# The order of two attention kinds inside one mixer: dilated groups first, latent groups last

## What is computed

```python
z = rmsnorm(x, mix_norm_ab) @ w_in_ab              # 672 latent columns | 2304 dilated columns
# latent attention (MLA), 8 heads
cq, ckv, k_rope = split(z[:, :672], [384, 640])
cq, ckv = rmsnorm(cq, q_norm), rmsnorm(ckv, kv_norm)
q = cq @ w_uq        # 8 heads x (64 plain + 32 turned by the rotary angles)
k_nope, v = ckv @ w_ukv                             # 8 heads x (64 | 64)
k = [k_nope, rope(k_rope) for every head]
o_a = softmax(q k^T / sqrt(96)) v                   # 512 columns
# dilated attention, 3 dilations x 4 slots
o_g, lse_g = softmax(q_g k_g^T / 8 + bias_g) v_g
o_b = sum_g softmax_g(lse) o_g                      # 256 columns
x = x + [o_a, o_b] @ w_out_ab
```

## Time and profile before

| | us |
|---|---|
| median of 3 runs | 2044.84 (2043.64 to 2045.15) |
| the profiled execution, its own time | 2039.9 |
| its span in the trace | 2038.1 |
| busy: PE | 1965.0 (96%) |
| busy: DVE | 1379.5 (68%) |
| busy: ACT | 838.4 (41%) |
| busy: POOL | 105.3 (5%) |

### The profile page before, as it was taken

One profiled execution on the slowest core, in us unless ns is written; L12 is line 12 of the kernel. 1 busy time (PEld: TensorE's weight loads), 2 busy tenths in 40 slices (PEclk: granted clock), 3 DMA queues, 4 the chain that ended last, 5 costly groups with the idle time before them and its releaser, 6 DMA issues.

```text
span 2038.1 us, 33547 instructions
## 1 busy us (share of the span) xinstructions
PE 1965.0 (96%) x12752; PEld 1773.3 (87%) x12752; DVE 1379.5 (68%) x1758; ACT 838.4 (41%) x1043; POOL 105.3 (5%) x130
## 2 busy tenths in 40 slices
PE   7989999989999999999999999999999999999998
PEld 7978888878888888899899988878888998998886
DVE  5477776766777776755576777777667457677776
ACT  4454333544333433334254343333334325534333
POOL 0002000410000000000100100000000002010000
PEclk9999999999999999999799999999999999999999
DMA  7503555414555555545333455565554443344553
GB/s 286 186 40 123 194 190 187 175 42 180 194 194 190 214 196 185 188 153 181 110 112 138 166 176 189 195 229 188 186 188 174 162 148 104 125 172 170 186 190 139
DMA packets 47761, 343.60 MB, mean 169 GB/s; under 512 B 5360, under 2 KB 5392, under 8 KB 7456
## 3 DMA queue, kind: packets, MB, share of 16 engines
q1 hardware_dynamic: 44784, 324.55, 44.4%
q0 software_dynamic: 2864, 17.46, 2.3%
HBM read 340.94 MB, written 1.05 MB: 168 GB/s over the span
## 4 chain that ended last, share of the span: by engine, by line
issue 65%; PE 28%; POOL 3%; DVE 3%; ACT 1%; DMA 0%; POOLq 0%; DVEq 0%; ACTq 0%
PE bank L820 8%; PE bank L704 4%; PE bank L706 4%; PE bank L705 4%; PE bank L819 4%; PE bank L763 1%; PE bank L895 1%; PE bank L871 1%; POOL rstd L596 1%; DVE y L1439 1%; POOL mix L694 1%; PE bank L822 0%; POOL gn L644 0%; POOL grs L596 0%; POOL rnorm L686 0%
## 5 line engine op out<-in xcount | busy, mean ns | idle before, releaser
L1402 DVE TENSOR_TENSOR wlo<-raw,whi 128x2048 fp32r<-128x2048 f32 x306 | 701.2, 2293 | 301.3 <-ACT whi L1110 300.2
L820 PE MATMUL bank<-ysp,whi 128*128 128x512 f32 x2112 | 731.8, 397 | 6.3 <-DVE ysp L1417 4.1
L1110 ACT ACTIVATE whi<-raw 128x2048 fp32r<-128x2048 f32 x307 | 586.2, 1909 | 283.9 <-PE bank L706 279.4
L819 PE MATMUL bank<-ysp,wlo 128*128 128x256 f32 x1848 | 516.1, 279 | 0.0
L820 PEld LDWEIGHTS bank<-ysp,whi 128*128 128x128 f32 x2112 | 382.1, 188 | 81.5 <-issue 6.0
L819 PEld LDWEIGHTS bank<-ysp,wlo 128*128 128x128 f32 x1848 | 349.2, 189 | 11.8
L1175 ACT ACTIVATE sg<-sg 128x256 f32<-128x256 f32 x132 | 55.2, 418 | 505.2 <-DVE sg L1496 505.2
L704 PE MATMUL bank<-ysp,wlo 128*128 128x256 f32 x720 | 210.3, 292 | 9.9 <-ACT gates L1343 8.0
L705 PE MATMUL bank<-ysp,whi 128*128 128x256 f32 x720 | 207.1, 288 | 0.0
L706 PE MATMUL bank<-ysp,whi 128*128 128x256 f32 x720 | 207.0, 287 | 0.0
L704 PE MATMUL bank<-whi,hl 128*128 128x512 f32 x528 | 205.6, 389 | 0.0
(11 more groups left out here) (292 smaller groups left out, 2415.3 us busy)
## 6 DMA issues: line engine op xcount, KB each, us to landing
raw<-stream SPq DMA_DIRECT2D x307, 1024.0 KB, 4.8
gbc<-gains POOLq DMA_DIRECT2D x11, 512.0 KB, 4.0
cw<-small POOLq DMA_DIRECT2D x2, 2048.0 KB, 10.8
dbias<-dilb POOLq DMA_DIRECT2D x1, 2304.0 KB, 10.2
lng<-rows POOLq DMA_DIRECT2D x2, 1024.0 KB, 5.2
tab<-second POOLq DMA_DIRECT2D x1, 1724.0 KB, 9.3
x<-xin SPq DMA_DIRECT2D x2, 512.0 KB, 6.6
out<-y SPq DMA_DIRECT2D x1, 1024.0 KB, 3.8
```

Source lines behind the costliest of these rows:

```text
L819: pe.matmul(o[:, 0, :], lo[:, k, cols], yh[:, k, :], start=False, stop=False, skip_group_check=True)
L820: last = pe.matmul(o, hi[:, k, cols], ysp[:, :, k, :], start=k == 0, stop=k == 7)
L1110: act.activation(whi[s], raw[s], ACT.Copy).then_inc(hi_made, 1)
L1402: dve.tensor_tensor(wlo[s], raw[s], whi[s].bitcast(F32), ALU.subtract).then_inc(lo_made, 1)
```

## The change

PE now runs the dilated groups first, right after `z`. The loop's `extra` on PE, `project(i)`, does one step of `uq` (i = 0 to 2) or of `ukv` (i = 3 to 6) between S(i) and T(i-1), each into bank 0 and each waiting for the drain of the step before it (`alone=True`); at i = 7 it transposes the queries. All seven steps are drained by ACT (`projected`), after exp(i) and ahead of ACT's copy of T(i-1). For `ukv` the drain is two instructions, keys straight into `kasm` and values into `mkv`. POOL spreads the turned shared key into `kasm`, once, early. DVE turns the queries at i = 4 and copies batches at i = 7. The splits of the weight tiles 14, 15 and 16 move into the loops: ACT's at i = 0, 3, 5 of the dilated loop, DVE's at i = 1 of it and at i = 0 and 3 of the latent one.

The four latent groups come last, with the halves of one set of four heads next to each other. Between them PE transposes what is finished of the output: the dilated columns after S(2), heads 0 to 3 ahead of T(3). These batches are copied by both engines, and stand in the same two banks as the T batches. Heads 4 to 7 are transposed after the first 24 matmuls of step 0 of `wout`.

```diff
-PLAN1.weights("uq", "DDD", 2)
+PLAN1.weights("uq", "AAA", 2)
 PLAN1.weights("ukv", "AAAA", 4)
+PLAN1.batches("dil", "ADADADADADAD")
 PLAN1.batches("mqk", "ADADADAD")
-PLAN1.batches("mla", "ADADADAD")
-PLAN1.batches("dil", "ADADADADADAD")
-PLAN1.batches("ocat", "BBB")
+PLAN1.batches("mla", "AD" "BAD" "AD" "BAD")
+PLAN1.batches("ocat", "B")
...
 # PE
+            def project(i):
+                if i == 0:
+                    copied(B, tb_cq + 3)
+                if i < 3:
+                    dense(B, "uq", i, "T", kc=3, ..., act=(cqTh, cqTl), per_tile=2, bank=0, alone=True)
+                elif i < 7:
+                    dense(B, "ukv", i - 3, "T", kc=2, ..., act=(kvTh, kvTl), per_tile=4, bank=0, alone=True)
+                else:
+                    pe.wait_ge(src_ready, 2)
+                    for b in range(4):
+                        batch(B, B.plan.tb["mqk"] + b, [mq[:, m, 2 * b + k, :] for k in range(2) for m in range(M)], DK1)
+            attention(B, "dil", dil_groups(), AG_DIL, project)
+            ... four batches of kasm ...
+            def heads_T(i):
+                if i == 1:
+                    keep_warm(7, 0)
+                if i == 2:
+                    pe.wait_ge(src_ready, 3)
+                    square(B, B.plan.tb["mla"] + 2, lambda m, k: ocat[:, m, 512 + k * P:512 + k * P + P], 2, 4)
+                if i == 4:
+                    pe.wait_ge(o_ready, AG_MLA + 2)
+                    square(B, B.plan.tb["mla"] + 7, lambda m, k: ocat[:, m, k * P:k * P + P], 2, 4)
+                if i == 5:
+                    keep_warm(4, 0)
+            attention(B, "mla", mla_groups(), AG_MLA, heads_T, MLA_TURNED)
...
+            tokens_in_order(B, tile, (4, 5, 0, 1, 2, 3), 4, (oTh, oTl), bank2(0), last_heads).then_inc(step_done, 1)
 # ACT
+            def group_weights(i):
+                if i in (3, 6):
+                    ... exp of the group weights ...
+                if i in (0, 3, 5):
+                    split(B, B.plan.tile["uq"] + {0: 2, 3: 3, 5: 4}[i])
+            def projected(i):
+                if i < 3:
+                    stepped(B, "uq", i)
+                    act.activation(mq..., bank2(0), ACT.Copy).then_inc(drain_act, 1)
+                else:
+                    stepped(B, "ukv", j)
+                    act.activation(kasm[:, :, 2 * j:2 * j + 2, 0:64], kv[:, :, :, 0:64], ACT.Copy)
+                    act.activation(mkv[:, :, 2 * j:2 * j + 2, 64:128], kv[:, :, :, 64:128], ACT.Copy).then_inc(drain_act, 1)
+            attention(B, "dil", dil_groups(), AG_DIL, group_weights, projected)
+            attention(B, "mla", mla_groups(), AG_MLA, after=heads_T, turned=MLA_TURNED)
 # DVE
+            def beside(i):
+                if i == 1:
+                    split(B, B.plan.tile["uq"] + 2)
+                if i == 4:
+                    queries_turned()
+                if i == 7:
+                    for b in range(4):
+                        plain_T(B, B.plan.tb["mqk"] + b, ...)
+            def heads_T(i):
+                if i in MLA_TURNED:
+                    ... lo_T of the turned batch ...
+                if i in (0, 3):
+                    split(B, B.plan.tile["wout"] + i // 3)
 # POOL
+            pool.wait_ge(kr_ready, 1)
+            for m in range(M):
+                ins = pool.tensor_copy(kasm[:, m, :, 64:96], kr[:, m, :].unsqueeze(1).broadcast_to([P, H1, 32]))
```

More of the change, by code:

```diff
@@ L494, in bank2, with turned_at @@
             return pb[i].rearrange("p (a n) -> p a n", a=2)
+        def turned_at(B, stage, groups, turned):
+            first_tb, t = [], B.plan.tb[stage]
+            for i, g in enumerate(groups):
+                t += turned.get(i + 1, 0)
+                first_tb.append(t)
+                t += g["nk"] // P
+            return first_tb
         def pt_part(g, b):
@@ L504, in mla_groups @@
             out = []
-            for m in range(M):
-                for q in range(2):
+            for q in range(2):
+                for m in range(M):
                     i = len(out)
@@ L509, in mla_groups @@
                     out.append(dict(
+                        needs=PLAN1.tb["mqk"] + 6 + 2 * q,
                         q=[mqT[0:DK1, h, m * P:m * P + P] for h in hs], k=[mkT[0:DK1, h, :] for h in hs],
@@ L617, in _ @@
             power(4)
+            pool.wait_ge(kr_ready, 1)
+            for m in range(M):
+                ins = pool.tensor_copy(kasm[:, m, :, 64:96], kr[:, m, :].unsqueeze(1).broadcast_to([P, H1, 32]))
+            ins.then_inc(kr_spread, 1)
             power(2)
@@ L744, in tokens, with tokens_in_order @@
                 return last
+            def tokens_in_order(B, tile, ks, held, act, o, late):
+                s = B.slot(tile)
+                hi, lo = rows3(whi[s], len(ks), 256), rows3(wlo[s], len(ks), 256)
+                for part in (ks[:held], ks[held:]):
+                    if part[0] == ks[held]:
+                        late()
+                    for m in range(M):
+                        t = slice(m * P, m * P + P)
+                        for k in part:
+                            last = three(o[:, m, :], (act[0][:, k, t], act[1][:, k, t]), (hi[:, k, :], lo[:, k, :]),
+                                         m == 0 and k == ks[0], m == M - 1 and k == ks[-1])
+                return last
             def copied(B, n):
@@ L854, in ffn, with attention @@
                 down(B, NF * f, NF // 2 - 1, FFN_TILES - 1)
[L856 to L861, removed]
+            def attention(B, stage, groups, ag0, extra=None, turned={}):
+                first_tb = turned_at(B, stage, groups, turned)
                 n = len(groups)
@@ L934, in _ @@
+            pe.wait_ge(drain_act, B.drained(B.plan.step["z"] + 12, "A"))
+            attention(B, "dil", dil_groups(), AG_DIL, project)
             tb = B.plan.tb["mqk"]
-            for b in range(4):
-                batch(B, tb + b, [mq[:, m, 2 * b + k, :] for k in range(2) for m in range(M)], DK1)
-            pe.wait_ge(src_ready, 3)
+            pe.wait_ge(drain_act, B.drained(B.plan.step["ukv"] + 4, "A"))
+            pe.wait_ge(kr_spread, 1)
             for b in range(4):
                 batch(B, tb + 4 + b, [kasm[:, m, 2 * b + k, :] for k in range(2) for m in range(M)], DK1)
-            copied(B, tb + 8)
@@ new lines, in _, with last_heads @@
+            attention(B, "mla", mla_groups(), AG_MLA, heads_T, MLA_TURNED)
+            tb = B.plan.tb["ocat"]
+            tile, step = B.plan.tile["wout"], B.plan.step["wout"]
+            def last_heads():
+                pe.wait_ge(o_ready, AG_GQA)
+                square(B, tb, lambda m, k: ocat[:, m, 256 + k * P:256 + k * P + P], 2, 4)
+                copied(B, tb + 1)
+            tile_split(B, tile)
+            bank_free(B, step, True)
+            copied(B, tb)
+            tokens_in_order(B, tile, (4, 5, 0, 1, 2, 3), 4, (oTh, oTl), bank2(0), last_heads).then_inc(step_done, 1)
@@ L951, in _ @@
+            for i in range(1, 4):
+                dense(B, "wout", i, "T", kc=6, act=(oTh, oTl))
             norm_T(B, "n1", 1)
@@ L1189, in ffn, with attention @@
                 ahead(B, stage, FFN_TILES - 1)
[L1191 to L1195, removed]
+            def attention(B, stage, groups, ag0, extra=None, after=None, turned={}):
+                first_tb = turned_at(B, stage, groups, turned)
                 n = len(groups)
@@ L1545, in bc, with attention @@
                 return a.unsqueeze(len(a.shape)).broadcast_to(list(a.shape) + [n])
[L1547 to L1551, removed]
+            def attention(B, stage, groups, ag0, drain, extra=None, before=None, turned={}):
+                first_tb = turned_at(B, stage, groups, turned)
                 n = len(groups)
@@ L1651, in _ @@
[L1651 to L1666, removed]
+            def queries_turned():
+                dve.wait_ge(drain_act, B.drained(B.plan.step["uq"] + 3, "A"))
+                qa, qb = mq[:, :, :, 64:80], mq[:, :, :, 80:96]
+                t = [rt[:, i, :].rearrange("p (m h f) -> p m h f", m=M, h=H1) for i in range(4)]
+                cb = cos1.unsqueeze(2).broadcast_to([P, M, H1, 16])
+                sb_ = sin1.unsqueeze(2).broadcast_to([P, M, H1, 16])
+                dve.tensor_tensor(t[0], qa, cb, ALU.mult)
+                dve.tensor_tensor(t[1], qb, sb_, ALU.mult)
+                dve.tensor_tensor(t[2], qa, sb_, ALU.mult)
+                link(dve.tensor_tensor(t[3], qb, cb, ALU.mult))
+                dve.tensor_tensor(qa, t[0], t[1], ALU.subtract)
+                dve.tensor_tensor(qb, t[2], t[3], ALU.add).then_inc(src_ready, 1)
@@ L1711, in _, with heads_T @@
             dve.wait_ge(dilb_in, 16)
-            attention(B, "mla", mla_groups() + dil_groups(), AG_MLA, drain,
-                      before=lambda i: weights((i - AG_DIL) // DG) if i >= AG_DIL and (i - AG_DIL) % DG == 1 else None)
-            square_T(B, B.plan.tb["ocat"], 3, oTl, oTh)
```

(11 more changed lines are left out.)

73 lines of the change are left out of this document (27 added, 46 removed).

## The result

The changed kernel is slower: 2055.3 us against 2044.1 (medians of six runs each), ratio 1.0056 with a 95% interval of 1.0041 to 1.0072. In a second set of runs it was 1.0080 (1.0058 to 1.0102). The forecast was 2048.8 with a range up to 2053, so the time lies outside it.

What follows compares the result with a forecast made beforehand. It took TensorE's waits between `uq` and step 0 of `wout` as all that the change touches: +0.8 us for the new order and +3.2 for two clock falls, +4.0 on the median of 2044.84, giving 2048.8 us, range 2042 to 2053.

Steps and rivals of the forecast that it cites:

- The walk: Step-by-step timing from `uq` to step 0 of `wout`: waits of 17.6 us, end at 170.9 against 170.1, +0.8 us.
- the first turned batch: Latent loop, output transposes: waits 1.6 us for a bank that ACT's copy of T(0) frees only after exp(1).
- T(1)'s second half: Latent loop: 2.4 us idle for the bank of the turned batch, whose copy stands behind exp(2).
- The second turned batch: Latent loop, heads 0 to 3 before V(2): 2.6 us idle for V(1)'s drain, behind DVE's second split.
- +2.8 at equal clocks: Stretch from `uq` to step 0 of `wout`: new order's cost over the old with slow clock left out, +2.8 us.
- The clock: Latent loop: two falls to 1.2 GHz, in low stretches 142.8 to 147.6 and 154.2 to 158.8, 3.2 us for both.
- the term of 3.2: Cost in us of the two expected clock falls in the latent loop, 1.2 to 2.0 each.
- Rival (c): Latent loop: slow clock lasts from 147.6 to 163.6 without being given back, +8 instead of 3.2, 2053 us; chance 0.14.
- The account of TensorE's work: Stretch from `uq` to step 0 of `wout`: 61.2 us plus 1.2 of warming matmuls, leaving 17.5 waits and slow clock before.
- Adding the difference to the median: Whole kernel: the +4.0 us, taken against the profiled execution (2039.9), was added to the runs' median, 2044.84.
- Rival (b): Dilated loop: the projection's drain isn't the pace, waits of 5.6 us shrink to about 1.0, 2040.3 us; chance 0.16.
- Rival (d): Behind the stretch: something else would hold `wout`, so nothing is moved, 2044.8 us; chance 0.03.

Runs made afterwards that it cites:

- fill_latent: Changed kernel plus 5, 10, 9 and 4 calls of matmuls without use in the latent loop's four waits: 2047.6 us, 1.0029 of the kernel before.
- set 2: Second of three timing sets: the kernel before (2043.4 us) beside the changed kernel again (2056.4 us, 1.0080) and three kernels with added matmuls without use.
- banks: Changed kernel with project(1) put into bank 1 and project(6) into bank 2: 2051.9 us, 1.0047 of the kernel before.
- late: Changed kernel with all three output transpose batches moved behind the latent loop: 2051.5 us, 1.0035 of the kernel before.
- warm_mla: Changed kernel plus 10, 20, 14 and 8 calls of matmuls without use in the latent loop's waits: 2051.9 us, 1.0038 of the kernel before.

## Why the prediction was wrong, point by point

- **The walk held.** project(1) started at 96.84 (forecast 96.8, wait 2.2 for 2.4); project(6) waited 1.9 for 2.1; project(4) and (5) 0.3 and 0.2 for 0.7 and 0.4; the first turned batch 1.3 for 1.6; T(1)'s second half 2.5 for 2.4, by the low part of the turned batch as stated; the last batch 1.5 for 1.5. The second turned batch waited 1.3 for 2.6, since at half rate V(1) ended later and hid more of the split. The first latent scores started at 138.56, 48.5 us after S(0) where I had 43 to 46; in fill_latent, without the two falls ahead of them, it is 45.4. "+2.8 at equal clocks" is best read from fill_latent, whose stretch has this order, no slow clock, and fillers that don't overrun the waits: 81.3 us against 79.9 - 1.7 = 78.2, so +3.1. That the column at full clock also gives 1.9 to 2.7 for the changed kernel is luck: by that split its stretch costs nothing (78.4), and in the profile the late wait of 1.6 us makes the difference.
- **The clock is the step that failed.** "I expect two falls [...] 1.2 to 2.0 each, 3.2 for both": the size wasn't right, and the places only roughly (151 and 165, both later than forecast). I took the length of the one fall before, 3.4 us, as the length of any. The profile had falls of 10.2 and 13.6 us in the latent loop and two more of 3.4 that I had not forecast, and the stretch ended at 183.8 where the walk without slow clock gave 170.9: the term of 3.2 measured 12.9. Against the kernel before, the changed kernel is 12.5 us shorter of clock in the means of set 2 (38.7 against 26.2), and fill_latent gave 8.8 us back by removing slow clock while adding work. Rival (c), slow clock that isn't given back, at 2053, came nearest; it too was short (+8), and the clock did come back for 3 us, at 161.5. It had 0.14, with rows of 20.5 and 6.9 us in the earlier trace rows that should have given it far more.
- **Two sums were off without harm.** The account of TensorE's work, 62.4 us, is some 4 us too small: before, TensorE was busy 68.6 us in the stretch, 1.7 of it slow clock. The waits were too large by as much in both orders (13.1 us measured for 17.6 in the new one), so the difference stood.
- **The filler's price.** Eleven calls at 0.11 are in the account of TensorE's work; they take 0.23. It cancels between the two orders, and cost two experiments their clean answer. It also makes the one fall before cost 1.7 us and not 2.0: four of the calls lie in the 5.2 us that I compared with 3.2.
- **A comparison with few runs.** The kernel before scatters from 2034 to 2048 us over the sets here, and its profiled execution (2039.9) lay below the medians, 2043.3 to 2044.8. Adding the difference to the median was right.
- Rival (b), the drain not being the pace, falls with the walk's waits as they came, and with banks, which halved them. Rival (d) falls with the changed kernel itself: the first dense matmul of the feed-forward step started at 203.6 us instead of 189.8, so the stretch's 13.8 us passed on in full.
- Of the Trainium skill's page TensorE: Matmul & The Clock Gate, "HAM oscillation" (only a long gap brings the low rate), the trace disagrees: the clock fell after waits of 2.2 and 1.9 us, and in late after one of 1.48. The same page's table of the two states has sustained work bring the full rate back; here 13.14 busy us of 13.80 stood at a clock of 0.51.

What stays open: why a fall in the latent loop lasts 10 to 17 us with TensorE busy, and the one at 156 us before, in the same T and V instructions, 3.4; why the waits of 2.2 and 1.9 us ahead of project(1) and (6) brought falls in the changed kernel and in late, and none in warm_mla and fill_latent, where they are as long; and why the new order brings the late wait at 1381 us.

## What to carry to other kernels

When an order is changed, count TensorE's idle stretches and also what runs right behind them: a wait of 1.3 to 2.5 us among small matmuls and transposes cost 5 to 8.5 us more in clock here (falls of 10.2 to 17 us), and the short falls 1.7 each. A copy that frees a shared bank mustn't stand behind the next group's exps; give the batch another bank or put it behind the loop. Matmuls without use in such waits gave 7 to 9 us back in two kernels here, 3 to 5 where I had their price wrong by half, and nothing clear in two others: read their real price from the trace first.

## What the runs showed of the hardware that I had not expected

- The low clock level can hold through continuous work: 13.6 us at 0.50 to 0.51 with TensorE busy 95% of it (64-column value matmuls, transposes and the fillers), given back 2.4 us after dense 256-column matmuls began at 176.1. Dense matmuls don't end it at once everywhere: in late it held 5.7 us into them, and in the kernel before, at 1006 us, 5.6.
- The kernel's time scatters with the clock: late ran from 2040.6 to 2055.8 us, with mean granted clocks from 0.990 to 0.979, and the kernel before from 2034.0 to 2048.2.
- A 128x128 fp32 matmul of the identity is two instructions and 0.23 us.
